# RWKV recursion on one core: every second block's target tokens in the other partition half, whole inverses from the doubling, and the solve moved to the slot's opening

## What is computed

```python
def _rwkv7_scan(r, decay, k, v, kk, a):
    # S_t = S_{t-1} (diag(w_t) - kk_t^T (a_t * kk_t)) + v_t^T k_t ;  y_t = S_t r_t.
    def step(S, inp):
        r_t, w_t, k_t, v_t, kk_t, a_t = inp
        sa = jnp.einsum('bhvk,bhk->bhv', S, -kk_t)
        S = (S * w_t[:, :, None, :]
             + sa[..., None] * (kk_t * a_t)[:, :, None, :]
             + v_t[..., None] * k_t[:, :, None, :])
        y = jnp.einsum('bhvk,bhk->bhv', S, r_t)
        return S, y
```

## Time and profile before

| | |
|---|---|
| median of 3 runs | 3517.65 us (3516.7 to 3517.87) |
| span of the profiled execution | 3515.1 us |
| instructions | 75244 |
| TensorE busy | 3295.0 us, 94% |
| VectorE busy | 2186.4 us, 62% |
| ScalarE busy | 1464.0 us, 42% |
| GpSimd busy | 560.4 us, 16% |

### The profile page before, as it was taken

How to read it: one execution, slowest core, us unless ns; L and a number is a source line. 1 busy time by engine, 2 the same in 40 slices (tenths; PEclk the granted TensorE clock), 3 DMA queues, 4 the chain that set the end, 5 groups by cost and what they waited for, 6 DMA issues and landing times. The chain is left out here.

```text
span 3515.1 us, 75244 instructions
## 1 busy us (share of the span) xinstructions
PE 3295.0 (94%) x31246; PEld 2822.4 (80%) x31246; DVE 2186.4 (62%) x3701; ACT 1464.0 (42%) x2121; POOL 560.4 (16%) x792
## 2 busy tenths in 40 slices
PE   7999999999699998989979979949999999999997
PEld 5778888788577786867868868839999999999997
DVE  4666766667445655677777766666565655565563
ACT  5445444444255655332232223424444444444442
POOL 3455555554100000000000000000100110011000
PEclk9999999999899999989999999959999999999999
DMA  4221222211233434422121245436666666666662
GB/s 145 56 83 51 66 74 62 83 49 46 66 126 109 149 125 140 137 73 72 62 70 61 84 136 176 157 105 219 215 200 214 203 213 204 215 203 210 207 215 72
DMA packets 361838, 452.90 MB, mean 129 GB/s; under 512 B 15188, under 2 KB 300148, under 8 KB 361588
## 3 DMA queue, kind: packets, MB, share of 16 engines
q1 hardware_dynamic: 350200, 407.40, 35.7%
q0 software_dynamic: 9216, 33.56, 4.1%
q10 hardware_dynamic: 2176, 8.39, 0.6%
HBM read 382.17 MB, written 67.13 MB: 128 GB/s over the span
## 5 line engine op out<-in xcount | busy, mean ns | idle before, releaser
L2840 PE MATMUL bank<-ex_x_hi,ex_w_lo 128*128 128x256 f32 x2048 | 581.5, 284 | 2.0 <-DVE ex_x_lo L3022 2.0
L2841 PE MATMUL bank<-ex_x_lo,ex_w_hi 128*128 128x256 f32 x2048 | 580.2, 283 | 0.0
L2842 PE MATMUL bank<-ex_x_hi,ex_w_hi 128*128 128x256 f32 x2048 | 580.1, 283 | 0.0
L2836 DVE TENSOR_TENSOR ex_w_lo<-ex_w_loaded,ex_w_hi 128x2048 fp32r<-128x2048 f32 x192 | 433.9, 2289 | 226.7 <-ACT ex_w_hi L2832 222.3
L2832 ACT ACTIVATE ex_w_hi<-ex_w_loaded 128x2048 fp32r<-128x2048 f32 x192 | 359.4, 1904 | 172.5 <-PE bank L2842 169.3
L2840 PEld LDWEIGHTS bank<-ex_x_hi,ex_w_lo 128*128 128x128 f32 x2048 | 393.4, 192 | 2.8 <-issue 2.2
L2841 PEld LDWEIGHTS bank<-ex_x_lo,ex_w_hi 128*128 128x128 f32 x2048 | 393.5, 192 | 0.6
L2842 PEld LDWEIGHTS bank<-ex_x_hi,ex_w_hi 128*128 128x128 f32 x2048 | 393.5, 192 | 0.0
L2316 PE MATMUL bank<-sc_tokens_hi,sc_w_lo 128*128 128x512 f32 x672 | 267.7, 398 | 38.7 <-DVE hidden_hT_split L2428 16.0
L2896 POOL CAST ex_idx<-moe_idx_all 128x2 uint32 (+1 forms) x16 | 3.0, 186 | 1760.9 <-POOLq L79 1449.6
L2318 PE MATMUL bank<-sc_tokens_hi,sc_w_hi 128*128 128x512 f32 x672 | 265.0, 394 | 0.0
(11 more groups left out here) (485 smaller groups left out, 8312.5 us busy)
## 6 DMA issues: line engine op xcount, KB each, us to landing
ex_w_loaded<-in_wg SPq DMA_DIRECT2D x64, 1024.0 KB, 5.5
ex_w_loaded<-in_wu SPq DMA_DIRECT2D x64, 1024.0 KB, 6.5
ex_w_loaded<-in_wd SPq DMA_DIRECT2D x64, 1024.0 KB, 5.0
plain_weights<-in_w_in SPq DMA_DIRECT2D x70, 512.0 KB, 4.6
gl_ada_tile<-in_ada_w SPq DMA_DIRECT2D x48, 512.0 KB, 4.3
hidden_first_w<-in_sc_w_in SPq DMA_DIRECT2D x24, 1024.0 KB, 5.1
plain_columns<-hT_dram SPq DMA_DIRECT2D x14, 1024.0 KB, 7.4
plain_columns<-in_x SPq DMA_DIRECT2D x16, 512.0 KB, 5.7
```

The source lines that it names most:

```text
L2836: nc.vector.tensor_tensor(w_lo[c % SPLIT][:], raw[:, c % LOADED, :], w_hi[c % SPLIT][:].bitcast(F32), ALU.subtract).then_inc(s["lo"], 1)
L2840: nc.tensor.matmul(psum, ll, rh, start=first, stop=False)
L2841: nc.tensor.matmul(psum, lh, rl, start=False, stop=False)
L2842: return nc.tensor.matmul(psum, lh, rh, start=False, stop=last)
```

## The change

The target tokens of group jj = 1 are put into the other partition half: chunk c of such a group goes to half 1 - c. The forms of the keys (`PR`, first form) are stored with their two chunks swapped for those groups, at the cost of three pieces in place of one in the exponent on ScalarE and in the product on VectorE. In `corner`, `double`, `inputs_of`, `solve` and `y_inside` problems with jj = 0 stay straight and those with jj = 1 go across, into neighbouring banks. `turn_y` swaps the halves back.

The unit matrix is added to E (VectorE, `keep_e`), so that the doubling yields the whole inverse, and ScalarE copies it (`keep_t`) in place of VectorE's two additions. `corner` and `inputs_of` write into banks 1 and 2; `inputs_of(g)` runs at the end of slot g, before `double(g, 4)`, and VectorE keeps it; `solve(b)` stands right behind `level(g, 0)`, and `turn(2f + 1)` between `level(g, 1)` and `double(g, 1)`. `y_inside` is cut in two. `turn_x` also waits for `wu_kept`. In the queues VectorE's `keep_final` and `keep_bonus` come after `keep_e(g, 0)` and `keep_solved(b)`; ScalarE's `keep_y(b)` comes before `keep_t(g, 4)`. GpSimd's `corner` makes the factors and the starting inverse by two instructions of four problems in place of five of two.

```diff
-        STRAIGHT, ACROSS = 5, 4
+        STRAIGHT, ACROSS = 4, 5
+        of_both = lambda first, a, z: k.psum[:].rearrange("p (i x) -> p i x", x=512)[:, first:first + 2, a:z]
+        rows_of = lambda jj, c: heads2[1 - c if jj else c]
+        def straight(p, l):
+            h, jj = p // 2, p % 2
+            return h == (jj if l % 2 == 0 else 0)
+        def lower_at(p, l):
+            return (0 if straight(p, max(l - 1, 0)) else 2) + p % 2
+        def upper_at(p):
+            return 2 * (p % 2) + p // 2
                 def double(g, l):
                     it = inv[g % 2]
+                    if l == 0:
+                        pe.wait_ge(s["t_turned"], g + 1)
                     pe.wait_ge(s["e_kept"], g * LEVELS + l + 1)
-                        for cr in heads2:
-                            nc.tensor.matmul(bank[STRAIGHT][cr, jj * P + C:jj * P + P], eb[cr, 1, jj, :], it[cr, near, 1, :], start=True, stop=True)
-                        for cr in heads2:
-                            mm = nc.tensor.matmul(bank[STRAIGHT][cr, 384 + jj * C:384 + jj * C + C], eb[cr, 0, jj, :], it[cr, far, 1, :], start=True, stop=True)
+                    for h in range(2):
+                        o = slice(h * P + C, h * P + P)
+                        for jj in range(2):
+                            p = 2 * h + jj
+                            for c in range(2):
+                                cr, to = heads2[c], rows_of(jj, c)
+                                mm = nc.tensor.matmul(bank[ACROSS if jj else STRAIGHT][to, o], eb[cr, 0 if straight(p, l) else 1, jj, :], it[cr, upper_at(p), 1, :],
+                                                      start=True, stop=True)
                     mm.then_inc(s["dt"], 1)
                 def corner(f):
                     pe.wait_ge(s["nt0"], f + 1)
-                    if f >= 2:
-                        pe.wait_ge(s["state"], 4 * (f - 2) + 5)
                 def inputs_of(b):
-                    pe.wait_ge(s["state"], 4 * b + 1)
+                    pe.wait_ge(s["sc_kept"], b + 1)
                 def solve(b):
                     pe.wait_ge(s["x_kept"], b + 1)
-                    pe.wait_ge(s["t"], 2 * (b + 1) * LEVELS)
+                    pe.wait_ge(s["t"], (b + 1) * LEVELS)
# TensorE's queue
                     if levels:
                         level(g, 0)
                     if back:
-                        inputs_of(b)
+                        solve(b)
                     if front:
                         turn(2 * f)
...
                     if levels:
                         level(g, 1)
-                    if back:
-                        solve(b)
+                    if front:
+                        turn(2 * f + 1)
                     if levels:
                         double(g, 1)
-                    if front:
-                        turn(2 * f + 1)
                     fill(i, half, 1)
...
                     if front:
                         corner(f)
                     if levels:
+                        inputs_of(g)
                         double(g, 4)
# ScalarE
-                def keep_e(g, l):
-                    act.wait_ge(s["e"], g * LEVELS + l + 1)
+                def keep_t(g, l):
+                    act.wait_ge(s["dt"], g * LEVELS + l + 1)
+                    which = slice(1 if l == LEVELS - 1 else 0, 2)
...
+                    if back:
+                        keep_y(b)
                     if levels:
-                        keep_e(g, 4)
+                        keep_t(g, 4)
                     if half == 0 and i < NT and i % HP:
                         keys(i)
-                    if back:
-                        keep_y(b)
                     pump(i, half, 4)
# VectorE
+                def keep_e(g, l):
+                    dve.wait_ge(s["e"], g * LEVELS + l + 1)
+                    nc.vector.tensor_tensor(eb[:], of_both(STRAIGHT, 256, 384).rearrange("p i (j t) -> p i j t", t=C), halves, ALU.add).then_inc(s["e_kept"], 1)
...
+                    if levels:
+                        keep_e(g, 0)
+                    if back:
+                        keep_solved(b)
                     if half == 0:
                         if 0 <= i - 4 < NT:
                             keep_final(i - 4)
                         if 0 <= i - 1 < NT:
                             keep_bonus(i - 1)
-                    if levels:
-                        keep_level(g, 0)
                     pump(i, half, 0)
-                    if back:
-                        keep_solved(b)
                     if levels:
-                        keep_level(g, 1)
+                        keep_e(g, 1)
                     pump(i, half, 1)
```

More of the change, by code:

```diff
@@ L349, in corner @@
                     pe.wait_ge(s["nt0"], f + 1)
-                    if f >= 2:
-                        pe.wait_ge(s["state"], 4 * (f - 2) + 5)
-                    for p, h, jj in pairs:
-                        for cr in heads2:
-                            mm = nc.tensor.matmul(bank[6][cr, p * C:p * C + C], nt0[cr, p, :], mk("halves")[cr, :], start=True, stop=True)
+                    for jj, (here, there) in of_level(0):
+                        o = slice(jj * C, jj * C + C)
+                        for c in range(2):
+                            nc.tensor.matmul(bank[1][heads2[c], o], nt0[heads2[c], here, :], mk("halves")[heads2[c], :], start=True, stop=True)
+                        for c in range(2):
+                            mm = nc.tensor.matmul(bank[2][heads2[1 - c], o], nt0[heads2[c], there, :], mk("halves")[heads2[c], :], start=True, stop=True)
                     mm.then_inc(s["corner"], 1)
@@ L375, in double @@
                     it = inv[g % 2]
+                    if l == 0:
+                        pe.wait_ge(s["t_turned"], g + 1)
                     pe.wait_ge(s["e_kept"], g * LEVELS + l + 1)
-                    for jj in range(2):
-                        near, far = jj, 2 + jj
-                        if l < LEVELS - 1:
-                            for cr in heads2:
-                                nc.tensor.matmul(bank[STRAIGHT][cr, jj * P:jj * P + C], it[cr, near, 1, :], eb[cr, 1, jj, :], start=True, stop=True)
+                    if l < LEVELS - 1:
+                        for jj, (here, there) in of_level(l):
+                            o = slice(jj * P, jj * P + C)
@@ new lines, in double @@
+                            for c in range(2):
+                                cr = heads2[c]
+                                nc.tensor.matmul(bank[ACROSS][heads2[1 - c], o], it[cr, upper_at(there), 1, :], eb[cr, 1, jj, :], start=True, stop=True)
+                    for h in range(2):
+                        o = slice(h * P + C, h * P + P)
+                        for jj in range(2):
+                            p = 2 * h + jj
+                            for c in range(2):
+                                cr, to = heads2[c], rows_of(jj, c)
+                                mm = nc.tensor.matmul(bank[ACROSS if jj else STRAIGHT][to, o], eb[cr, 0 if straight(p, l) else 1, jj, :], it[cr, upper_at(p), 1, :],
+                                                      start=True, stop=True)
@@ L389, in double @@
                     mm.then_inc(s["dt"], 1)
                 def inputs_of(b):
[L392 to L395 removed]
+                    pe.wait_ge(s["sc_kept"], b + 1)
+                    for h in range(2):
+                        o = slice(128 + h * C, 128 + h * C + C)
+                        for jj in range(2):
+                            for c in range(2):
+                                cr, to = heads2[c], rows_of(jj, c)
+                                mm = nc.tensor.matmul(bank[1 + jj][to, o], scm[b % 3][cr, 2 * h + jj, 2, :], tm[b % 3][cr, jj, 3, heads2[h]], start=True, stop=True)
@@ L502, in _ @@
                         transfer(b)
+                        y_inside(b, 0)
                     if levels:
                         double(g, 2)
+                    fill(i, half, 2)
                     if back:
-                        y_inside(b)
-                    fill(i, half, 2)
+                        y_inside(b, 1)
                     if levels:
@@ L1134, in _ @@
                         chunk(b, 3)
+                    if levels:
+                        keep_e(g, 4)
                     if front:
```

184 lines of the change are left out of this document (97 added, 87 removed).

## The result

The changed kernel takes 3557.6 us (median of 4 runs, 3554.2 to 3563.1), the kernel before 3517.2 beside it: a ratio of 1.012, interval 1.0107 to 1.0132. The change makes the kernel 1.2% slower, 40 us; 3500.6 was forecast, with 3523 as the upper end. The profiled execution has a span of 3552.2 us against 3515.1.

The account below looks back on a forecast made before the run. The prediction took TensorE (94% busy) as the bound in slots with products, and waits between stages in the tail. Savings less stalls, plus blocks 0 and 1 and the tail, summed to 17 us: 3517.65 to 3500.6 us, range 3474 to 3523.

Parts of the forecast that it names:

- TensorE's savings: Four positions in double, corner, inputs_of and solve save 2.0 us per block, net 1.7 after a moved turn.
- The three stalls: TensorE would idle before turn_y (0.65 us), the decay job (1.2) and level 0's double in second slots (1.2 or 2.3).
- Gate into `turn_y`: ScalarE's keep_t(g,4) waits for double and precedes keep_block, so turn_y comes 0.65 us late in every tile.
- Bonus into the decay job: VectorE's bonus, now behind E and keep_solved, delays the decay job 1.2 us; 0.15 where i % 4 = 2 or 3.
- E of level 0 in second slots: VectorE's weighed keys ahead of E stall double 1.2 us, 2.3 with keep_lo; none for i % 4 = 0.
- The walk: Each engine's queue followed through one tile like i = 13 with the rows' durations; assumed error 1 us per tile.
- The collision: L887 on VectorE, starting behind GpSimd's L1149, takes 2.47 us instead of 0.55 in eleven of sixteen tiles.
- Tiles 14 and 15: Counted with i = 5, 9, 13, each gaining 0.5 us after a 1.25 us stall on E of level 0.
- Tiles 4, 8, 12: Gain 0.3 us each after waits on bonus (0.9), lora tanh (0.9), E of level 1 (1.0) and gate (0.65).
- The states: Because chunk(b,2) already waits for chunk 1's state, shorter double(g,3) gains 0.1 us, not 0.23; y_inside unchanged.
- The tail: Blocks 29 to 31, without products: shorter TensorE levels, one addition less, a longer copy, shorter GpSimd corner; 5 us gained.
- slower: Rival, chance 0.14: the collision takes all three VectorE weighing instructions and keep_lo, 3 us a tile in eleven tiles, 3534.

Follow-up runs that it names:

- runs 12 and 14: Reordered kernel (VectorE's work spread, keep_lo in third part) with all solve matmuls straight, into two banks or one: 3489.7 and 3489.9 us, one execution each.
- run 10: Reordered kernel (VectorE's work spread, keep_lo in third part) with straight matmuls before crossed in double's second line, corner, inputs_of, solve: 3484.6 us, ratio 0.9911.
- run 3: Changed kernel with ScalarE's product evacuations, lora tanh and, where i % 4 = 0, decay tanh in front of keep_t: 3532.7 us, ratio 1.0048.
- run 4: Changed kernel with VectorE's keep_bonus in front of keep_e(g,0) and keep_solved in first slots: 3546.3 us, ratio 1.0092; outputs use a later tile's bonus.
- run 5: Changed kernel with TensorE's state outputs reordered, second half of chunk 1's output ahead of chunk 2's state wait: 3550.0 us, ratio 1.0099.
- run 13: Reordered kernel (VectorE's work spread, keep_lo in third part) with two tail orders put back as in the changed kernel: 3471.4 us, ratio 0.9886.
- run 1: Changed kernel with VectorE's normalise, weigh_keys (i % 4 > 0) and keep_lo behind keep_e(g,0) and keep_solved of the next slot: 3550.7 us, ratio 1.0100.

## Why the prediction was wrong, point by point

- **TensorE's savings: right in the main.** `solve` starts its sixteen records over 0.35 us (forecast 0.44 less the last step), `inputs_of` starts 0.23 us behind `corner`, `double` takes 0.48 instead of 0.70. The reason given, two positions against four, is the one that runs 12 and 14 bear out; that they must alternate is not (run 10). Blocks 0 and 1, where little else acts, gained 2.5 us, as forecast. One step fell short: `double(g, 4)` starts 0.82 us behind `corner`, where the sum had 0.46 and 0.1 for the wait on E of level 4. That wait is under-sized by a quarter of a microsecond in each slot, some 7 us.
- **The three stalls: right in place.** Gate into `turn_y`: 0.65 us, as forecast, and run 3 removes it. Bonus into the decay job: 1.1 (forecast 1.2), and run 4 gives 0.8 of it back. E of level 0 in second slots: named, and under-sized.

Set against the groups of the sum, in us (a minus is a gain):

| group | forecast | measured |
|---|---|---|
| blocks 0, 1 | -2.5 | -2.5 |
| i = 5, 9, 13 | -1.5 | +4.4 |
| i = 14, 15 | -1.0 | +9.7 |
| i = 2, 3, 6, 7, 10, 11 | -6 | +14.4 |
| i = 4, 8, 12 | -1 | +11.3 |
| tail | -5 | -1.3 |

- **The step that failed: the price of the stall on E of level 0, and first of all the clock behind it.** The walk charged the stall alone, at full clock. The TensorE clock falls behind seven of these eleven stalls and in tiles 4, 8 and 12, 41 us at half speed where the kernel before has none in slots 0 to 28. By run 3's pair of slots that is an estimated 19 us, the largest term of the miss, and the sum had nothing for it. The stall itself was too small as well: 1.6 to 1.7 us of idle TensorE instead of 1.25 where no subtraction follows, 2.6 to 3.2 instead of 2.3 with `keep_lo`, 3.0 and 3.2 instead of 1.25 in tiles 14 and 15. Added up that is 28.9 us instead of 20. In block 24 `keep_e` starts 5.5 us behind the first matmul of the last product half (759.36 to 764.88), where the walk had 5.1. `keep_inputs` (L1099, 0.42 us) stands where two additions stood, so `normalise` starts only 0.15 us earlier behind that matmul than before, 0.59 instead of 0.74.
- **The collision: right in size and direction, wrong in its victim.** The walk let it hit L887, at 2.47 us. GpSimd's split did move earlier in VectorE's order, as the walk said: it now starts 0.2 us behind `normalise`, where it started 0.2 behind L886. So the next instruction in line is caught, which is L946, the kk_a product, and L947, the old L887, takes 0.55 in all tiles. The extra time is the same, 2.0 us in L946 and 1.9 in the old L887; in tiles 11 and 14 `normalise` is caught, 0.02 us behind the split, and the stall is 0.2 us longer. The Trainium skill has this kind of victim in the very section that the prediction drew on (SBUF — State Buffer, Who interferes with whom): a VectorE instruction with two SBUF inputs contends with a GpSimd instruction that reads SBUF. The trace agrees: L946 reads two tensors in SBUF and took 2.1 to 2.8 us in the nine tiles, 0.7 to 0.8 in the others. The prediction used only the rule on 2-port modes beside it, and it cost it nothing.
- **Tiles 14 and 15: put in the wrong group.** They were counted with i = 5, 9, 13 at a gain of 0.5. They carry the subtractions for the next phase where other tiles carry `keep_lo`, and lost 9.8 us in their second slots: some 11 us of the error.
- **Tiles 4, 8, 12: forecast +0.3 gain each, measured 3.8 loss.** I had listed the waits on bonus, lora, E of level 1 and gate. The waits on the keys' block (0.61) and on the decay tanh before r's product (0.91) were not in the list, since I followed `keep_t` only where a job was next and not for each evacuation behind it. Run 3 takes 4.0 us off each first slot, the half clock there included. 12 us of the error.
- **The states: a term of the wrong sign.** Level 3 to level 4 was to become about 0.1 us shorter; it became 0.6 (first slots) and 0.7 (second) longer. `y_inside(b, 1)` now ends just ahead of `chunk(b, 0)`, whose wait for it shows as a start 0.50 and 0.66 us after level 3 instead of 0.28, and chunk 3 waits for its own first output (0.55 us instead of 0.17). Both waits stand in the changed kernel; the prediction took `y_inside` as unchanged and priced neither. Part of it, 0.15, is only shifted, since level 3 starts that much earlier among the last matmuls of `y_inside`. In the 25 slots of blocks 1 to 28 outside the first slots of tiles 4, 8 and 12 it is 16.6 us, and most of the miss in i = 5, 9 and 13, where the pair of slots went from 51.2 to 52.6 instead of down by 0.5. Run 5 gets 0.2 a slot back.
- **The tail:** 5 us forecast, 1.3 measured. Orders made for slots with products cost there; run 13 shows 4.1 against before.

The rival *slower* had the place (E of level 0 behind a longer VectorE queue) and the sign, and 3534 for a time, and it was given 0.14. Its mechanism did not come: one instruction is slowed in each tile, as in the forecast itself, and not three. The sign set down for it, E of level 0 more than 2.5 us late without `keep_lo`, showed in tiles 14 and 15 alone; in i = 5, 9 and 13 it was less, and these tiles lost 1.5 us each all the same, most of it by the states. What the sum lacked besides was the clock, the states and ScalarE's order, and no rival stood for these. These misses overlap in the slots, so they are not summed; the tables are the account. The split of the loss between stall, clock and states is read from slots and one pair of them, not from an edit that moves one alone.

## What to carry to other kernels

When an operation that TensorE waits for moves to another engine, it inherits that engine's whole queue, collisions included: a slow instruction that was free the day before stands on the path. Then look first at what stands ahead of the moved operation and which other engine starts beside it; here one order and one wait turned the same matmuls from 1.2% slower to 0.4% faster, and with VectorE's work spread and the tail set right it was 1.1%. And price each wait line in a diff, also those that an engine has for its own results. Price a stall of TensorE at more than its length: here the clock fell behind many of them, and in run 3's pair of slots that cost 1.6 us on top of a stall of 1.6.

## What the runs showed of the hardware

- Eight f32 matmuls of 64x128 in 64x64 positions (sixteen records) that all go straight start two records at a time, over 0.773 us, into one bank or two. Half straight and half crossed they start four at a time, over 0.35 us when alternating; with four straight ahead of four crossed it is 0.40.
- A VectorE instruction with two SBUF operands that starts while GpSimd's subtraction of 1024 elements a row (2.4 us) runs ends after it, by 0.55 us in the first two cases and 1.07 in the third: the kk_a product took 2.1 to 2.8 us instead of 0.8, `normalise` 2.9 instead of 0.7 to 0.8, `keep_lo` in run 1 (1024 elements a row) 3.4 instead of 1.3. `normalise` started 0.2 to 0.3 us ahead of GpSimd's took 0.8; then GpSimd's own took 2.8 instead of 2.4 and the next VectorE instruction was caught. 0.01 to 0.02 us behind it, `normalise` was the one.
- Behind 3.2 us of idle TensorE (block 20) the granted clock was 0.50 for 3 us; behind 1.63 us (block 24) it stayed at 1. The length of the stall does not decide it alone: in run 3 the clock stayed behind 1.63 us (block 8) and fell behind 1.64 (blocks 16 and 24), and it stayed behind stalls of some 3 us in blocks 12 and 20. In tile 12 two shorter stretches, 1.24 and 0.61 us around the two decay jobs from 692.8 us, were followed by 0.50 from 697 to 700, where the matmuls of `scores` started over 1.4 us instead of 0.9.
